# Order of the query tiles in differential attention: 1, 4, 2, 3 key tiles in place of 1, 2, 3, 4

## The reference, cut to what matters

```python
q = rotary(...)   # 2*8 heads of 64: two score maps for each of 8 heads
k = rotary(...)
s = einsum('bhqd,bhkd->bhqk', q, k) * 64 ** -0.5
s = where(key position <= query position, s, -inf)
att = softmax(s, axis=-1).reshape(b, 8, 2, q, k)
w = att[:, :, 0] - lam * att[:, :, 1]
out = einsum('bhqk,bhkd->bhqd', w, v)          # v: 8 heads of 128
out = rms_norm(out, subln) * (1.0 - lambda_init)
return out @ w_o
```

## Time and profile before

| what | value |
|---|---|
| median of 3 runs | 3074.11 us (3073.71 to 3075.41) |
| the profiled execution's own time | 3073.34 us |
| its span | 3071.3 us |
| PE busy | 2830.5 us, 92% of the span |
| DVE busy | 1580.5 us, 51% |
| ACT busy | 1148.3 us, 37% |
| mean granted PE clock | 0.951 of full speed |

### The profile page before, as it was taken

How to read it: one execution, slowest core, us unless ns; L and a number is a source line. 1 busy time by engine, 2 the same in 40 slices (tenths; PEclk the granted TensorE clock), 3 DMA queues, 4 the chain that set the end, 5 groups by cost and what they waited for, 6 DMA issues and landing times.

```text
span 3071.3 us, 34951 instructions
## 1 busy us (share of the span) xinstructions
PE 2830.5 (92%) x12976; PEld 2000.6 (65%) x12976; DVE 1580.5 (51%) x1995; ACT 1148.3 (37%) x1502; POOL 265.3 (9%) x232
## 2 busy tenths in 40 slices
PE   6988899999999999999799679999998988999998
PEld 3856665555455545655387468888886756888887
DVE  5557644555555545565454445434455566444445
ACT  3242313444454434454332124222343256322334
POOL 1064720100010001100100000000000000000000
PEclk8997989999999999999889789999999989999999
DMA  7244849999999999999932022333332201333210
GB/s 227 75 134 172 279 162 395 393 393 392 395 395 390 396 396 360 394 392 396 384 111 90 28 96 87 92 103 93 100 96 74 84 22 29 92 92 104 89 55 28
DMA packets 220355, 620.92 MB, mean 202 GB/s; under 512 B 19638, under 2 KB 38084, under 8 KB 219316
## 3 DMA queue, kind: packets, MB, share of 16 engines
q1 hardware_dynamic: 204528, 565.12, 50.2%
q0 software_dynamic: 11552, 41.94, 4.9%
q10 hardware_dynamic: 4100, 11.59, 1.0%
HBM read 590.52 MB, written 28.05 MB: 201 GB/s over the span
## 4 chain that ended last, share of the span: by engine, by line
PE 68%; DMA 10%; DVE 9%; SPq 7%; ACT 3%; issue 2%; DVEq 0%; ACTq 0%; POOLq 0%
PE ps L273 66%; SPq L450 6%; DMA ring<-in_w_gu 5%; DMA ring<-in_w_down 3%; DVE arena L193 2%; PE ps L289 2%; ACT wunits L463 1%; ACT arena L238 1%; DVE arena L204 1%; DVE ring_r L473 1%; DVE arena L212 1%; DVE arena_r L204 1%; DMA arena<-in_w_gu 1%; DMA arena<-in_ctx 1%; DMA sum_scratch<-arena 1%
## 5 line engine op out<-in xcount | busy, mean ns | idle before, releaser
L273 PE MATMUL ps<-arena_r,wunits 128*128 128x512 f32 (+1 forms) x3552 | 1110.9, 394 | 15.6 <-DVE arena_r L193 7.7
L473 DVE TENSOR_TENSOR ring_r<-ring,wunits 128x1024 fp32r<-128x1024 f32 (+1 forms) x491 | 588.5, 1219 | 715.9 <-ACT wunits L463 661.3
L463 ACT ACTIVATE wunits<-ring 128x1024 fp32r<-128x1024 f32 (+1 forms) x491 | 508.0, 1049 | 802.9 <-PE ps L273 654.9
L273 PEld LDWEIGHTS ps<-arena_r,wunits 128*128 128x128 f32 x3552 | 670.6, 190 | 165.7 <-issue 15.8
L273 PE MATMUL ps<-arena_r,ring_r 128*128 128x512 f32 (+1 forms) x1776 | 694.9, 391 | 0.0
L273 PE MATMUL ps<-wunits,arena_r 128*128 128x512 f32 x1792 | 517.5, 402 | 28.8 <-ACT wunits L463 28.5
L273 PEld LDWEIGHTS ps<-wunits,arena_r 128*128 128x128 f32 x1792 | 332.9, 189 | 131.5 <-issue 32.7
L273 PEld LDWEIGHTS ps<-arena_r,ring_r 128*128 128x128 f32 x1776 | 337.3, 190 | 70.6
L273 PE MATMUL ps<-arena 128*64 128x512 f32 (+12 forms) x1652 | 301.1, 436 | 52.9 <-DVE arena L208 21.2
L273 PE MATMUL ps<-ring,arena 128*64 128x512 f32 (+1 forms) x1256 | 323.9, 605 | 12.3 <-issue 5.7
L273 PEld LDWEIGHTS ps<-arena 128*64 128x64 f32 (+5 forms) x1652 | 161.0, 185 | 173.0 <-issue 84.6
(11 more groups left out here) (178 smaller groups left out, 1872.5 us busy)
## 6 DMA issues: line engine op xcount, KB each, us to landing
ring<-in_w_gu SPq DMA_DIRECT2D x370, 512.0 KB, 15.8
ring<-in_w_down SPq DMA_DIRECT2D x166, 512.0 KB, 17.4
arena<-in_w_gu SPq DMA_DIRECT2D x142, 512.0 KB, 15.8
arena<-in_w_down SPq DMA_DIRECT2D x90, 512.0 KB, 16.5
ring<-in_w_ada SPq DMA_DIRECT2D x48, 512.0 KB, 5.7
ring<-in_ffn_w_gate SPq DMA_DIRECT2D x44, 512.0 KB, 3.7
ring<-in_ffn_w_up SPq DMA_DIRECT2D x44, 512.0 KB, 3.8
ring<-in_ffn_w_down SPq DMA_DIRECT2D x40, 512.0 KB, 3.6
```

The source lines that it names most:

```text
L273: ins = self.e.matmul(o, l_, r_, start=start, stop=stop, skip_group_check=True)
L463: q.inc(q.e.activation(h, raw, ACT.Copy), (st.tag, "hi", i))
L473: q.inc(q.e.tensor_tensor(lo, raw, h.bitcast(F32), ALU.subtract), (st.tag, "lo", i))
```

## The change

The units keep their numbers, and a table gives each its query tile: positions 0, 1, 2, 3 of a head take the tiles of size 1, 4, 2, 3. All pieces of a unit follow. The work of `head_act` (squares of the head before, copy of the finished head) stays tied to the position in the head. The buffers still alternate with u % 2 and u % 3. The tile of size 1 is still first, so the start of the accumulation stays with it. No instruction is added or removed, and no DMA is moved.

```diff
+    ROWS = (0, 3, 1, 2)
+
     def scores_pe(p, u):
-        h, i = u // 4, u % 4
+        h, i = u // 4, ROWS[u % 4]
...
     def masked_pe(p, u):
-        i = u % 4
+        i = ROWS[u % 4]
...
     def exps_dve(v, u):
-        i, q, p = u % 4, u % 2, u % 3
+        i, q, p = ROWS[u % 4], u % 2, u % 3
...
     def exps_act(q, u):
-        i, b, p = u % 4, u % 2, u % 3
+        i, b, p = ROWS[u % 4], u % 2, u % 3
...
-        p, nk = u % 3, (u % 4 + 1) * 128
+        p, nk = u % 3, (ROWS[u % 4] + 1) * 128
...
     def turned_pe(p, u):
-        i, q, x = u % 4, u % 2, u % 3
+        i, q, x = ROWS[u % 4], u % 2, u % 3
...
     def turned_act(q, u):
-        i, p = u % 4, u % 2
+        i, p = ROWS[u % 4], u % 2
...
     def values_pe(p, u):
-        h, i, q = u // 4, u % 4, u % 2
+        h, i, q = u // 4, ROWS[u % 4], u % 2
...
-        h, i = u // 4, u % 4
-        if h and i < 2:
-            head_sum(q, h - 1, 2 * i)
-            head_sum(q, h - 1, 2 * i + 1)
-        if i == 3:
+        h, n = u // 4, u % 4
+        if h and n < 2:
+            head_sum(q, h - 1, 2 * n)
+            head_sum(q, h - 1, 2 * n + 1)
+        if n == 3:
```

## The result

The changed kernel takes 3085.28 us (median of 7 runs, 3080.81 to 3086.33). The kernel before took 3075.41 us on the same chip (7 runs, 3072.97 to 3080.38). The ratio is 1.0031 with a 95% interval of 1.0021 to 1.0041, so it is slower by 0.3%, some 9.5 us. The forecast was 3081.5 in a range of 3074.5 to 3087.5. The profiled execution took 3084.45 us with a span of 3082.5, 11.2 above the span before.

What follows compares the result with a forecast made beforehand. A loop of waits through PE, DVE and ACT was taken to bound the attention. Loops 2.7, ends 1.1 and clock 3.8 made 7.6 us on 3073.34, 3080.9; with the median's 0.8, 3081.7, forecast as 3081.5, range 3074.5 to 3087.5.

Steps and rivals of the forecast that it cites:

- The loop of a head: Attention, new order: tiles of size 4 and 3 share one wait loop, 11.50 us at full clock, 0.39 more per head.
- The loop before: Attention, old order: loop from one size-4 maximum to the next, through ACT's own queue, 11.11 us at full clock.
- E4: Exponentials of the size-4 tile on ACT, a term of 1.68 us in the old and new loops.
- E2: Exponentials of the size-2 tile on ACT, a term of 1.25 us in ACT's own queue.
- hidden pair loop of 10.5: Old order: wait loop coupling tiles of size 4 and 2, some 10.5 us, hidden 0.6 below the 11.11.
- The ends: Attention's start and tail: 3.8 us gained before the first size-4 tile, 4.9 lost after the last, 1.1 cost.
- The clock: PE in the attention: one costly low-clock stretch per loop, 7.0 us over seven loops against 3.2 now, 3.8 more.
- The sum: Whole change: 2.7 for the loops, 1.1 for start and tail, 3.8 for low clock, 7.6 us slower.
- The clock costs no more than now: Rival: the loop is right but low clock on PE adds nothing; 3.8 us above, 3078; chance 0.27.
- Faster: Rival: ACT's copies do not hold back PE's long blocks, ACT's queue sets 10.76 a head; 3068 us; chance 0.08.
- Each loop is hit twice: Rival: low-clock stretches hit both long PE blocks; 3089 us at the bound, 3086 for three in two loops; chance 0.15.

## Why the prediction was right, step by step

**The loop of a head: right, to the hundredth.** Forecast 11.50 at the full clock, measured 11.50 in the changed kernel (there at a mean clock of 0.94), 11.51 twice in the order 1, 3, 2, 4, and 11.50 or 11.51 six times with PE filled. It is shown to be the pair that makes it: of four orders the two that couple 4 with 3 have it, their chain goes through the pair term by term, and with C ahead of E on ACT the same order has heads of 10.30.

**The loop before: right.** 11.11 or 11.10 with filling, six times, and with C ahead of E, which shortens ACT's way from E4 to C4, 10.22 to 10.24. The view of waits enters C4 from T1 instead (2512.70 to 2512.83), for which C4 does not wait by the kernel; ACT's last part of E2 ended at 2512.76 and C4 began at 2512.86. The way over PE is shorter by the 0.70 that V4 waits for C4. The hidden pair loop of 10.5 was not seen by itself. The order 1, 4, 3, 2 has the same pair and takes 10.77 by another way, DVE's queue, which neither confirms nor contradicts it. This way of DVE is the one that the prediction lacked: it called DVE hidden because of its 8.6 us of work, and did not add up the loop R4 to W3 with T and V behind it. For the changed kernel nothing hangs on it, since the 11.50 is longer.

**The ends: right in kind, undersized.** Forecast 1.1, measured 2.5. The gain at the start is as forecast (2.34 to the first tile of size 4, 2.35 estimated). In the tail I took the step R4 to R3 at the full clock, 5.72. It took 2572.49 - 2565.61 = 6.88, since the block of V3 and S3 fell on a low stretch there too (3.16). The rest, 8.35 from R3 to the reciprocal, was put at 8.1. With PE filled the step is 5.72, as forecast, and the ends differ by 1.3 (16.37 against 15.11). So the size was right at the full clock, and what it left out is the low stretch.

**The clock: shown, and right in size with some luck.** Forecast 7.0 for the seven loops of the changed kernel against 3.2, a difference of 3.8. By the full-clock loop it is 87.38 - 7 * 11.50 = 6.9 against 3.2, a difference of 3.7. The filling, which keeps its first loop long, gives back 6.0 and 2.1, a difference of 3.9. The reason given holds as well. In the loop of 2503.63 to 2515.13 the mean clock was 0.94 and the loop still took 11.50, since the low part lay on V2 and S2, which are not on it (1.89 in place of 1.46). In the other five behind the first loop the whole excess lies on one block of the chain: V4 with S4 in the second loop (3.38 in place of 2.45), V3 with S3 in the others (3.46, 3.20, 2.37 and 3.47 in place of 2.01). The size came about in another way than forecast. I took 1.0 in each of seven loops, and the seven excesses are 1.47, 0.93, 0, 1.46, 1.19, 0.37 and 1.46. One hit costs up to 1.46, and one loop has none. The first loop is a case of its own: its clock was 0.50 throughout, and the kernel before has an excess of 1.34 there too, so it adds next to nothing to the difference. That the sum is 6.9 against 7.0 is therefore in part luck.

**The sum.** Forecast 7.6 in the attention, measured 8.9 in the profile and about 9.5 by the ratio. The difference to the 8.9 is the tail; the step from 8.9 to 9.5 is within what single profiles and the interval leave open.

**The rivals.** "The clock costs no more than now" is refuted by the filling. "Faster" named the place that decides it: E4 finished before PE is through T1. In the changed kernel T1 is issued at 2506.15 and C3 behind E4 only at 2506.77, so PE waits 0.83, and the case does not arise. The experiment on ACT takes the copies out from behind the exponentials, and then the head is shorter by 1.2 us. "Each loop is hit twice" did not come: no loop behind the first had more than one block of the chain slowed. (The 3086 given there for three hits in two loops is 3085 by its own terms, 3074.1 + 3.8 + 10.5 - 3.2.)

The Trainium skill (TensorE: Matmul & The Clock Gate, "A second HAM failure mode: psum-queue depth-cycling") says that short idle times of PE between groups of matmuls make its clock go to and fro and cost throughput. The traces agree: with no single wait of PE above 1.18 us the mean clock of the changed kernel's loops was 0.83, and with the waits filled it was 1.00 in six of seven.

## What to carry to other kernels

In a software pipeline over units of unequal size, write down which unit each wait in every queue ties to which, and add up the loops that these ties close: here every other unit was coupled, so an order that looked more even from one unit to the next put the two largest into one loop. An engine's queue ties units together as firmly as a semaphore does, and moving one short instruction (a copy, ahead of exponentials that it does not need) was worth 14 us to the changed kernel (1.0031 to 0.9985), where the order had cost 9.5. Add up each engine's own queue with its gaps as well: where the loop of 11.50 was gone, the pace was mostly set by DVE's queue, alone (9.88) or with T, V and S behind it (10.77, 10.70, 10.30), although DVE was busy for only 8.6. If PE has idle time to spare, filled with harmless products it tells what the clock costs, and the loop stands bare.

## What was not expected of the hardware

Two heads with the same PE work and the same instructions took 11.87 and 12.96 us at a mean clock of 0.86 and 0.87: what a low stretch costs depends on where it falls. A shorter loop can lose it all: the order 1, 4, 3, 2 has 10.77 at the full clock and 11.72 in the mean (82.07 / 7). Also, 18 to 20 added passes of 128 columns in idle time of PE left the length of a head unchanged to 0.01 us and raised its clock to 1.00 in every head but the first. Why that first loop stays long (12.36 and 12.16) was not tried. The filling begins only with the fifth turn, and whether that is the reason is not shown.
